# Issuing the tensor engine's fp32 transposes as transpose operations in a two-block transformer kernel

## The chip, the cores and the metric

One NeuronCore of one Trainium2 chip runs the whole program; the other cores are idle. The metric is the device time in microseconds (us), the median over several executions.

## What is computed

The reference chains two small transformer programs over 256 tokens of width 1024, batch 1, all in fp32. The first has a gated delta rule layer and then a layer of sparse attention with three branches (compressed, selected and window keys); the second has a stick-breaking attention, a gated linear recurrence and two MLPs with squared ReLU. Cut to the order of the work:

```python
def first_block(x, c, ...):
    h = rmsnorm(x, norm_g[0]) * (1 + scale) + shift
    x = x + gate * gated_deltanet_layer(h, ...)
    shared = nsa_shared_kv(x, ...)
    h = rmsnorm(x, norm_g[1]) * (1 + scale) + shift
    x = x + gate * nsa_layer(h, shared, rel_bias, ...)
    return rmsnorm(x, final_g)

def second_block(x, ...):
    x = x + stick_breaking_attention(rms_norm(x, g0), w_qkv, w_o)
    x = x + squared_relu_mlp(rms_norm(x, g1), w1, w2)
    x = x + rglru_block(rms_norm(x, g2), ...)
    x = x + squared_relu_mlp(rms_norm(x, g3), w1, w2)
    return rms_norm(x, norm_final)
```

In `nsa_layer` each of 16 heads computes, in two branches, scores q kᵀ plus a bias, a masked softmax p and the product p v. At 256 tokens the selected branch sees every block and the window covers the sequence, so both are plain causal attention over 256 keys.

## The kernel before

The tokens lie on partitions in two tiles of 128. Every weight matrix is streamed from HBM in blocks of 1 MB (128 x 2048 fp32) through three raw buffers. ScalarE writes a rounded high part (L537, `split_hi`) and VectorE the remainder (L994, `split_lo`), into two split buffers; every weight product is then three TensorE products, high by high, high by low and low by high (`passes`, L1576, whose products are recorded at L1579 to L1581). A `feature_block` has 48 such products of 256 columns, a pair of `token_blocks` calls 48 of 512 columns. Each engine runs its own program in a fixed order written out by hand, and the engines meet at counting semaphores; there is no planner.

**Transposes.** `transpose` (L1573) is used for all of them: it is a matmul with the data as the stationary operand and the fp32 identity as the moving one. The calls are:

- `transposes(call)` (L1626), ten times: the normalised activations `xn` (2 x 128 x 1024) become feature-major in four PSUM banks, 16 transposes of 128x128. The first token tile's eight wait for the first `xn_ready`, the second tile's eight for the second. As the pairs of the second tile end (`tr_done`), ScalarE writes the high part hT_hi (`transposed_hi`, L561, recorded at L571, L578 or L580), VectorE the remainder hT_lo (`transposed_lo`, L1036, recorded at L1042 or L1048, and L1063), and the weight products wait for hT_lo (`fresh`, L1594). The calls are named h0, y0, kv, h1, y1, sb, o2, m0, rg and m1.
- in the delta rule stage, for each of two groups of four heads, 8 of v, 4 of k and 8 of the matrices `ddT` (L1727, L1735, L1746), in all 40.
- 4 small ones of `few` (L1676), 4 of `hid_rows` (L1852) and 4 of the compressed branch's weights `pc` (L1936).
- `weights_T(h)` (L1904): 6 of 128x128 for each of the 16 heads of the sparse attention, 96 in all: the exponentials `pr` become `pT`.

That is 160 + 40 + 12 + 96 = 308 transposes.

**The sparse attention's turn.** TensorE does for head h, in this order: the scores of head h + 1 (`scores`, L1892, recorded at L1900 and L1901, 64 partitions deep), the transposes of head h, and the products p v of head h - 1 (`head_out`, L1915, recorded at L1927 to L1929, 64 columns wide). Meanwhile VectorE adds the bias to the scores and takes the row maximum (L1342, L1345), ScalarE the exponentials (L801, `p_ready`); after the transposes ScalarE copies the first branch's result (L810) and VectorE the second's (L1385) to SBUF.

```python
for h in range(BH):
    if h + 1 < BH:
        scores(h + 1)
    weights_T(h)
    if h >= 1:
        head_out(h - 1)
```

Of the kernel before, what the change touches and what calls it, by code (L numbers as in the profile page):

```python
# [205 lines left out]
def build(nc, I, O):  # L206
# [11 lines left out]
    with ExitStack() as ctx:  # L218
# [1350 lines left out]
        def _(pe):  # L1569
            taken = [0]  # L1570
            dt32 = nc.tensor.matmul

            def transpose(out, x, one):  # L1573
                return dt32(out, x, one, start=True, stop=True)  # L1574

            def passes(out, lhs, rhs, first, last):  # L1576

# [48 lines left out]
            def transposes(call):  # L1626

                for m in range(MT):
                    pe.wait_ge(S["xn_ready"], XN[call] - 1 + m)
                    for g in range(4):  # L1630
                        bank = TR_BANK[g]
                        for c in range(2):
                            k = 2 * g + c
                            ins = transpose(bank[:, c * T + m * P:c * T + (m + 1) * P], xn[:, m, k * P:(k + 1) * P], ident)
                        if m == MT - 1:
                            ins.then_inc(S["tr_done"], 1)
# [30 lines left out]
            def few_columns(call, n):  # L1667

                _, hi, lo = take()
                for k in range(KC):  # L1670
                    fresh(call, k)
                    ins = passes(G[0][0:n, 0:T], (hi[:, k, :], lo[:, k, :]), hT(k), k == 0, k == KC - 1)
                ins.then_inc(S["w_used"], 1)
                pe.wait_ge(S["few"], 1 if call == "h0" else 2)
                for m in range(MT):
                    ins = transpose(G[1][:, m * n:(m + 1) * n], few[0:n, m * P:(m + 1) * P], ident[0:n, 0:n])  # L1676
                ins.then_inc(S["few_T"], 1)
# [38 lines left out]
            for hg in range(2):  # L1716
# [8 lines left out]
                for m in range(MT):  # L1725
                    for h in range(4):
                        ins = transpose(quad(X[m])[:, h, :], vT[:, 4 * hg + h, m * P:(m + 1) * P], ident)  # L1727
                    ins.then_inc(S["v_tok"], 1)
# [113 lines left out]
            for b in range(6):  # L1842
# [12 lines left out]
                if b == 1:  # L1855
# [7 lines left out]
                    for g in range(BG):  # L1863
                        for j in range(2):
                            ins = dt32(TB[1][0:NCMP, g * HD:(g + 1) * HD], hid[1][:, j, g * NCMP:(g + 1) * NCMP], cw2[1][:, j, :],
                                       start=(j == 0), stop=(j == 1))
# [261 lines left out]
```

## Time and profile before

| what | us |
|---|---|
| median of 3 runs | 1271.9 (1269.74 to 1272.17) |
| span of the profiled execution, first to last instruction | 1274.7 |
| the profiled execution's own time | no other than its span is recorded |
| TensorE matmuls busy | 1148.2 (90%) |
| TensorE weight loads busy | 1032.5 (81%) |
| VectorE busy | 701.8 (55%) |
| ScalarE busy | 567.5 (45%) |
| TensorE clock granted, mean | 0.936 of full |

Busy times are of one profiled execution. Matmuls overlap each other in the records, so their busy time is not the engine's throughput: that is read from start to start. A product of fp32 data is recorded as two weight loads and two matmuls, a product of the split parts as one of each, so the 308 transposes are 616 records. The granted clock is 1.00 at 2.4 GHz and 0.50 at 1.2 GHz.

### The profile page before, as it was taken

How to read it: one execution, taken by the hardware profiler on the slowest of the kernel's cores; microseconds unless marked ns; L12 is line 12 of the kernel's file. 1: busy time of each engine (PE TensorE's matmuls, PEld its weight loads, DVE VectorE, ACT ScalarE, POOL GpSimd, SP SyncE). 2: the span in 40 equal slices, each digit the busy share in tenths (PEclk: the TensorE clock that was granted, in tenths of full speed). 3: DMA queues.
4: the chain of work that ended last, by engine and by line, in shares of the span. 5: the costliest groups of instructions: out<-in, count | busy, mean ns of one | idle time of the engine just before them, and what ended most of it. 6: DMA issues, size and time to landing. Idle time of an engine off the chain costs nothing. (4 is left out here: it accounts for less than half of the span.)

```text
span 1274.7 us, 17755 instructions
## 1 busy us (share of the span) xinstructions
PE 1148.2 (90%) x7548; PEld 1032.5 (81%) x7548; DVE 701.8 (55%) x983; ACT 567.5 (45%) x837; POOL 90.1 (7%) x87
## 2 busy tenths in 40 slices
PE   2799978786989999998799998999999988999997
PEld 2699878785878786787599677989897976999896
DVE  5598455557544564355634345554555766654544
ACT  3354342323544443243543454434435585444343
POOL 1000016160000000031000001000000010000000
PEclk9798989897989997698999799999999998999999
DMA  9755405052335774000335303455556425455551
GB/s 328 226 165 167 133 11 188 2 198 71 102 103 169 236 255 166 1 1 1 111 109 179 131 1 113 144 178 195 182 183 197 133 99 165 135 197 180 186 197 66
DMA packets 118319, 178.45 MB, mean 140 GB/s; under 512 B 5125, under 2 KB 77987, under 8 KB 118241
## 3 DMA queue, kind: packets, MB, share of 16 engines
q1 hardware_dynamic: 116736, 172.40, 41.6%
q0 software_dynamic: 1088, 2.96, 0.7%
q10 hardware_dynamic: 416, 1.97, 0.4%
q8 instruction: 59, 0.97, 0.3%
q14 instruction: 20, 0.16, 0.0%
HBM read 176.27 MB, written 1.05 MB: 139 GB/s over the span
## 5 line engine op out<-in xcount | busy, mean ns | idle before, releaser
L994 DVE TENSOR_TENSOR sb_w_lo<-sb_raw,sb_w_hi 128x2048 fp32r<-128x2048 f32 (+2 forms) x141 | 319.4, 2265 | 348.9 <-ACT sb_w_hi L537 348.7
L537 ACT ACTIVATE sb_w_hi<-sb_raw 128x2048 fp32r<-128x2048 f32 (+2 forms) x141 | 266.1, 1888 | 177.9 <-PE G L1581 166.1
L1579 PE MATMUL X<-sb_hT_hi,sb_w_hi 128*128 128x256 f32 x1056 | 303.7, 288 | 3.0 <-DVE sb_hT_lo L1048 2.3
L1580 PE MATMUL X<-sb_hT_lo,sb_w_hi 128*128 128x256 f32 x1056 | 301.5, 285 | 0.0
L1581 PE MATMUL X<-sb_hT_hi,sb_w_lo 128*128 128x256 f32 x1056 | 301.4, 285 | 0.0
L1579 PEld LDWEIGHTS X<-sb_hT_hi,sb_w_hi 128*128 128x128 f32 x1056 | 205.2, 194 | 4.9 <-issue 4.1
L1580 PEld LDWEIGHTS X<-sb_hT_lo,sb_w_hi 128*128 128x128 f32 x1056 | 205.1, 194 | 0.6
L1581 PEld LDWEIGHTS X<-sb_hT_hi,sb_w_lo 128*128 128x128 f32 x1056 | 205.0, 194 | 0.0
L1579 PE MATMUL G<-sb_w_hi,sb_hT_hi 128*128 128x512 f32 x288 | 114.8, 398 | 10.2 <-DVE sb_hT_lo L1533 9.2
L1580 PE MATMUL G<-sb_w_lo,sb_hT_hi 128*128 128x512 f32 x288 | 113.5, 394 | 0.0
L1581 PE MATMUL G<-sb_w_hi,sb_hT_lo 128*128 128x512 f32 x288 | 113.5, 394 | 0.0
L1581 PE MATMUL G<-sb_w_hi,sb_uT_lo 128*128 128x512 f32 x256 | 101.1, 395 | 0.0
L1580 PE MATMUL G<-sb_w_lo,sb_uT_hi 128*128 128x512 f32 x256 | 101.1, 395 | 0.0
L1579 PE MATMUL G<-sb_w_hi,sb_uT_hi 128*128 128x512 f32 x256 | 101.0, 395 | 0.0
L1579 PEld LDWEIGHTS G<-sb_w_hi,sb_hT_hi 128*128 128x128 f32 x288 | 54.9, 191 | 23.0 <-issue 11.1
L868 ACT ACTIVATE sb_ur<-X 128x512 f32<-128x512 f32 x32 | 19.1, 598 | 106.5 <-PE X L1581 106.5
L1581 PEld LDWEIGHTS G<-sb_w_hi,sb_hT_lo 128*128 128x128 f32 x288 | 54.8, 190 | 11.6
L1580 PEld LDWEIGHTS G<-sb_w_lo,sb_hT_hi 128*128 128x128 f32 x288 | 55.0, 191 | 11.1
L1574 PE MATMUL T<-sb_consts,sb_xn 128*128 128x128 f32 x160 | 31.0, 356 | 32.2 <-DVE sb_xn L1023 20.8
L1581 PEld LDWEIGHTS G<-sb_w_hi,sb_uT_lo 128*128 128x128 f32 x256 | 48.2, 188 | 11.2
L1580 PEld LDWEIGHTS G<-sb_w_lo,sb_uT_hi 128*128 128x128 f32 x256 | 48.3, 188 | 10.7
L1579 PEld LDWEIGHTS G<-sb_w_hi,sb_uT_hi 128*128 128x128 f32 x256 | 48.3, 189 | 10.6
(346 smaller groups left out, 1682.9 us busy)
## 6 DMA issues: line engine op xcount, KB each, us to landing
sb_raw<-in_mlp_w SPq DMA_DIRECT2D x64, 1024.0 KB, 5.3
sb_raw<-in_ada_w SPq DMA_DIRECT2D x24, 1024.0 KB, 5.1
sb_raw<-in_a_in_w SPq DMA_DIRECT2D x16, 1024.0 KB, 5.9
sb_raw<-in_b_in_w SPq DMA_DIRECT2D x16, 1024.0 KB, 5.4
sb_raw<-in_sb_w_qkv SPq DMA_DIRECT2D x12, 1024.0 KB, 5.1
sb_raw<-in_rg_w_in SPq DMA_DIRECT2D x8, 1024.0 KB, 5.3
sb_raw<-in_a_out_w SPq DMA_DIRECT2D x4, 1024.0 KB, 4.9
sb_raw<-in_b_out_w SPq DMA_DIRECT2D x4, 1024.0 KB, 5.2
```

The costliest lines, as they stand in the source:

```text
L537: nc.scalar.activation(w_hi[s][:, 0:nk * w], raw[b % RAW_SLOTS][:, 0:nk * w], ACT.Copy).then_inc(S["w_hi"], 1)
L868: nc.scalar.activation(ur[b % 2][:, :, :], X[(f0 + b) % 2][:, :].rearrange("p (c t) -> p c t", c=2), ACT.Relu).then_inc(S["fm_out"], 1)
L994: nc.vector.tensor_tensor(w_lo[s][:, 0:nk * w], raw[b % RAW_SLOTS][:, 0:nk * w], w_hi[s][:, 0:nk * w].bitcast(F32), ALU.subtract).then_inc ...
L1574: return dt32(out, x, one, start=True, stop=True)
L1579: dt32(out, lh, rh, start=first, stop=False)
L1580: dt32(out, lh, rl, start=False, stop=False)
L1581: return dt32(out, ll, rh, start=False, stop=last)
```

## The change

The helper issues the tensor engine's transpose operation, with the same output, the same data and the same identity. Nothing else differs: the order, the waits, the buffers, and the copies out of PSUM.

```diff
--- before.py
+++ after.py
@@ -1571,7 +1571,7 @@
             dt32 = nc.tensor.matmul
 
             def transpose(out, x, one):
-                return dt32(out, x, one, start=True, stop=True)
+                return nc.tensor.transpose(out, x, one)
 
             def passes(out, lhs, rhs, first, last):
 
```

## Rows read from the trace of the kernel before

**Rows 1.** The page: span, and each engine's busy time.

```profile
span 1274.7 us, 17755 instructions
...
PE 1148.2 (90%) x7548; PEld 1032.5 (81%) x7548; DVE 701.8 (55%) x983; ACT 567.5 (45%) x837; POOL 90.1 (7%) x87
```

**Rows 2.** The instructions of line 1574: count, shortest/median/longest in ns, first and last start.

```profile
L1574 PE MATMUL T<-sb_consts,sb_pr x192: 274/276/581, 515.5 to 591.6; 128*128 128x128 f32 x192
...
L1574 PE MATMUL T<-sb_consts,sb_xn x160: 275/377/582, 31.9 to 1083.8; 128*128 128x128 f32 x160
...
L1574 PE MATMUL T<-sb_consts,sb_pc x8: 420/421/566, 500.8 to 502.5; 128*120 128x128 f32 x8
```

**Rows 3.** Busy time by stretch, line 1574 alone: stretch, length, PE, PEld, clock, DMA.

```profile
0.00:1274.70 1274.70, 100.95 (x616) 94.17 (x616) 0.94 0.43 140
```

**Rows 4.** Busy by stretch, sparse attention: length, PE, PEld, DVE, ACT, POOL, clock, DMA.

```profile
512.90:533.40 20.50, 20.50 (x79) 17.65 (x79) 5.78 (x30) 6.70 (x27) 0.00 (x0) 0.50 0.00 1
533.40:547.00 13.60, 13.60 (x103) 12.23 (x102) 8.32 (x39) 4.47 (x18) 2.41 (x2) 1.00 0.01 2
...
550.50:553.90 3.40, 3.40 (x19) 3.40 (x17) 0.56 (x2) 2.23 (x9) 0.00 (x0) 0.50 0.00 0
553.90:594.50 40.60, 39.27 (x296) 35.40 (x295) 21.96 (x103) 18.37 (x73) 11.45 (x12) 1.00 0.00 1
```

**Rows 5.** The same stretches, line 1574 alone: length, PE, PEld, clock, DMA.

```profile
512.90:533.40 20.50, 8.78 (x36) 7.90 (x36) 0.50 0.00 1
...
553.90:594.50 40.60, 14.42 (x108) 12.73 (x108) 1.00 0.00 1
```

**Rows 6.** TensorE's matmuls in order of time, two turns: start, length, operation, count.

```profile
521.25 2.93 PE L1574 MATMUL T<-sb_consts,sb_pr 128*128 128x128 f32 x12
523.97 0.53 PE L1927 MATMUL X<-sb_vtok,sb_pT 128*128 128x64 f32 x2
...
526.56 0.79 PE L1900 MATMUL G<-sb_kdup,sb_qB 64*128 64x128 f32 x2
...
529.42 2.93 PE L1574 MATMUL T<-sb_consts,sb_pr 128*128 128x128 f32 x12
...
573.12 1.60 PE L1574 MATMUL T<-sb_consts,sb_pr 128*128 128x128 f32 x12
...
577.44 1.61 PE L1574 MATMUL T<-sb_consts,sb_pr 128*128 128x128 f32 x12
```

**Rows 7.** Busy by stretch, stick-breaking attention's start; columns as in rows 4.

```profile
714.00:735.00 21.00, 19.36 (x58) 13.84 (x58) 7.09 (x11) 9.39 (x16) 0.00 (x0) 0.51 0.20 68
```

**Rows 8.** Order of time: products of split parts, 128x128 by 128 columns, ten in a row.

```profile
352.10 0.28 PE L1581 MATMUL X<-sb_w_hi,sb_hT_lo 128*128 128x128 f32 x1
...
353.11 0.28 PE L1581 MATMUL X<-sb_w_hi,sb_hT_lo 128*128 128x128 f32 x1
```

**Rows 9.** Order of time: the bf16 products of 16 columns at the start.

```profile
22.08 7.03 PE L1646 MATMUL G<-sb_rbx,sb_hot 97*128 97x16 bf16 x256 [22.08 <-DVE sb_rbx L1082]
```

**Rows 10.** Order of time: the transposes of call y0 and what surrounds them.

```profile
301.02 2.36 DVE L1222 TENSOR_TENSOR sb_xn<-sb_xn,sb_zs 128x1024 f32<-128x1024 f32 x2
...
302.30 2.08 PE L1574 MATMUL T<-sb_consts,sb_xn 128*128 128x128 f32 x8 [6.00 <-DVE sb_xn L1222]
...
305.88 1.92 PE L1574 MATMUL T<-sb_consts,sb_xn 128*128 128x128 f32 x8
307.04 1.63 ACT L578 ACTIVATE sb_hT_hi<-T,sb_params 128x256 fp32r<-128x256 f32 x4 [8.37 <-PE T L1574]
...
309.00 0.47 PE L1579 MATMUL G<-sb_w_hi,sb_hT_hi 128*128 128x512 f32 x1
```

**Rows 11.** Busy by stretch, columns as in rows 4: y0, then products after a pause.

```profile
304.70:308.10 3.40, 3.40 (x18) 3.40 (x18) 2.21 (x4) 1.06 (x3) 1.01 (x2) 0.50 0.43 132
308.10:311.50 3.40, 3.32 (x18) 2.72 (x18) 3.40 (x9) 2.03 (x6) 0.00 (x0) 0.99 0.56 217
1055.60:1059.00 3.40, 3.40 (x8) 2.72 (x9) 2.94 (x5) 2.35 (x3) 0.00 (x0) 0.50 0.68 266
```

## The prediction

> **What bounds the kernel now.** I read the page first: TensorE has 1148.2 us of recorded matmul in a span of 1274.7, far ahead of VectorE and ScalarE [rows 1]. So a shorter TensorE instruction is worth something wherever TensorE isn't waiting. The view of line 1574 gives the transposes: the 128x128 ones last 275 ns at their shortest, and the calls on xn have a median of 377 ns, so many of them run at the lower clock [rows 2]. All 616 records hold 100.95 us [rows 3]. That is the size of the prize; the question is how much of it is on the path, and what else these records do.
>
> The largest piece is the sparse attention, 512.9 to 594.5, 81.6 us with 192 of the records. TensorE is recorded busy nearly without a break, VectorE and ScalarE are busy about half the time or less [rows 4]: TensorE bounds it. The same rows show the second thing to see. In its first 20.5 us TensorE is busy for all 20.50, and yet the granted clock is 0.50, 1.2 GHz; then it is 1.00, falls once, and stays at 1.00 to the end. One turn (a head's transposes, the products of the head before, the scores of the head after) takes 529.42 - 521.25 = 8.17 us at the low level and 577.44 - 573.12 = 4.32 at the high one [rows 6]. The clock is worth more here than the transposes.
>
> **What one transpose costs.** Now: 12 records from 521.25 to 523.97, so 2.72 / 6 = 0.453 us per transpose at the low level; at the high level 1.60 us less the 0.275 of the last record, over 11 steps, is 0.12 per record, 0.24 per transpose [rows 6, 2]. The operation itself stands nowhere in this trace. The nearest rows are the products of split parts with the same 128x128 operand of four-byte data and the same 128 columns, one record each: ten in a row start 1.01 / 9 = 0.112 us apart, at the high clock [rows 8]. The low end is the bf16 products, 7.03 / 256 = 0.027 [rows 9]; the high end is 0.24, no change (nothing excludes a price above it, but no row suggests one). I take the nearest row, one record per transpose: 0.112 high, 0.225 low, so 0.227 us saved at the low level and about 0.12 at the high one.
>
> The Trainium skill (TensorE: Matmul & The Clock Gate, Terms) says that a transpose mode makes fp32 four times faster; an estimate by it is 0.113 low and 0.06 high, and would put my time some 11 us lower. No row here shows it.
>
> **The clock in the attention.** What raised it? Not recorded busy time: it was full for 20.5 us at 0.50 [rows 4]. The stick-breaking attention, which has no transposes but the same kind of products, 64 partitions deep or 64 columns wide, likewise runs 21 us at 0.51 with TensorE busy for 19.36 [rows 7]. In the sparse attention the rise at 533.4 comes just after the transposes that begin at 529.42 [rows 4, 6], the only products of the turn that are both 128 deep and 128 wide, 2.72 of its 8.17 us. In call y0 the clock is 0.50 through the transposes and 0.99 right behind them [rows 11]. My reading is that the transposes, as ordinary matmuls, are what brings the clock up in these places. After the change they last half as long and stream fewer passes; what is left of a low turn (2.59 us of narrow products from 523.97 to 526.56, 2.86 of shallow ones to 529.42) is what kept the clock down in both stages. The stage starts low today, so I expect it to stay low to its end.
>
> At the low level the turn becomes 8.17 - 6 x 0.227 = 6.81 us. The stage holds 16 transpose groups, 16 groups of products and 15 of scores: 16 x 6.81 - 2.86 = 106.1, against 81.6 now: **+24.5**. The exponentials can't bind at such a turn: VectorE and ScalarE have 5.78 and 6.70 us of work in 20.5 us [rows 4].
>
> The Trainium skill (the same page, Part 4: PE-mode transpose) says that the full clock does not engage for transpose mode, which does not count as busy in the same way; by it the +24.5 stands whatever the operation's length. It is the rule that speaks against this change, and no run here shows it yet.
>
> **The ten calls on xn.** In y0 the second tile's xn is ready at 303.39, but its transposes start at 305.88, behind the first tile's [rows 10]. After the change the first eight end at 302.30 + 8 x 0.225 = 304.10, hT_hi starts at 304.10 + (1.16 - 0.45) = 304.8 in place of 307.04, and the chain to the first product at 309.00 moves with it: 2.2 us. The bound for any low call is 10 x 0.227 = 2.3, for a high one 1.2. Six calls start at the low level (y0, kv, y1, sb, m0, rg); I take 1.8 each, because in some the second tile's xn or a weight split on ScalarE comes later. o2 and m1, high, give 0.8 each, h0 and h1 nothing: they wait for the modulation or the split. Sum -12.4.
>
> Against that, in these six the first product now finds the clock up [rows 11]; the transposes did the warming. Where products start cold, at 1055.60, they stay at 0.50 for 3.4 us [rows 11], and half of that, 1.7, is lost. Where the first ones come one by one behind hT_lo they may lose more; I take 2.3 each, 13.8. In o2 and m1 the clock is up today because transposes bridge the pause before the products; a shorter bridge may let it fall, and I charge 1.5 each. Together 16.8 - 12.4: **+4.4**. So the calls, which look like the safe part, give back what they gain.
>
> **The rest.** The four transposes of pc are at the low level [rows 2], on the path: -0.9. The 40 of the delta rule stage save up to 2 us where TensorE is waited for, and cost as much where the product levels behind ddT then start low: 0, within 2. The eight of few and hid_rows are not worth a term. No DMA, wait or queue moves. SP's weight prefetch is three buffers deep and follows the splits; where TensorE is later it only gains slack.
>
> **Sum.** 24.5 + 4.4 - 0.9 = +28.0 on the profiled execution, 1274.7 to 1302.7 of span. That execution is 2.8 us over the median of the runs; the same +28.0 on 1271.9 gives 1299.9, so 1300.
>
> **Rivals.**
>
> *The clock doesn't care (faster).* The mechanism is TensorE's path alone: shorter transposes at the clock pattern of today. Of 192 records 36 are in the first stretch [rows 5]: 18 x 0.227 + 78 x 0.12 = 13.5 us in the attention, 12 after turns that then wait for the exponentials; 12.4 in the calls, 0.9 and 2 elsewhere: 27.3 less, 1244.6. It decides if the attention reaches and holds 1.00, that is, if its turns fall under 4 us. For it: the clock did hold at 1.00 for 40.6 us, where transposes are 14.42 of 39.27 us busy [rows 4, 5], not the larger part. Against it: rows 4 and 7 at 0.50 with TensorE full. The Trainium skill (Perfetto Trace Analysis, Transposes) advises the transpose over a matmul; that is this rival's view. Chance 0.14. A milder form, the attention up but the calls paying as above, gives -12 + 4.4 - 0.9 = -8.5, 1263.4; chance 0.10.
>
> *The operation takes as long as now and the clock follows as now:* no change, 1271.9, chance 0.06. This is also the case that the operation is the same product under another name.
>
> *As long as now, but without the effect on the clock (much slower):* 16 x 8.17 - 2.86 = 127.9, +46.3, and 16.8 in the calls: 1335. Chance 0.04.
>
> The forecast has 0.66. Its own range: with the bf16 price at the low level, 0.055, the turn is 8.17 - 2.72 + 0.33 = 5.78 and the stage 89.6 (+8.0), the calls give another us or so each, and the whole is about 1275; the other end is the 1335. Inside these I hold 1280 to 1320 for it.
>
> **How the numbers follow.** A difference under 0.2%, 2.5 us, can't be told from none. Slower 0.66 + 0.04 = 0.70, same 0.06, faster 0.24. To leave out no more than 2 in 10 the range must take in the fast rival: 1243 to 1320.
>
> **What would show it.** Line 1574 with 308 records in place of 616, and steps of about 0.11 and 0.22 us. The attention at 0.50 from end to end, with turns of 6.8 us and a length near 106. The first product of the six calls 1 to 2 us sooner after xn, but at 0.50. The MLP stretches unchanged. I am wrong if the attention's clock reaches 1.00 and stays: then the turn is near 3.7 and the time near 1245 to 1263. I am also wrong in the terms, if not in the sign, if a transpose's step isn't 0.11.

## The result, and the profile after

| | before | after |
|---|---|---|
| median of 4 runs, beside each other | 1272.0 us (1269.7 to 1272.4) | 1282.8 us (1279.2 to 1285.8) |
| ratio | | 1.0111, interval 1.0064 to 1.0159 |
| span of the profiled execution | 1274.7 us | 1284.0 us |
| granted clock, mean | 0.936 | 0.900 |

The change makes the kernel slower by 1.1%, about 11 us. The sign and the place are those forecast; the amount is less than half of the 28 us. The four runs of the kernel before that stand beside it lie at its usual median; in other runs it took down to 1260 us (below), and against those the same change costs 21 us.

The page of the changed kernel, its span and busy times:

```profile
span 1284.0 us, 17139 instructions
...
PE 1148.2 (89%) x7240; PEld 1025.2 (80%) x7240; DVE 699.8 (55%) x983; ACT 567.1 (44%) x837; POOL 90.1 (7%) x87
```

308 records fewer than in [rows 1], and the same busy time to the tenth: what the shorter transposes took away, a slower clock put back. Line 1574 in it (count, shortest/median/longest in ns, first and last start):

```profile
L1574 PE MATMUL T<-sb_consts,sb_pr x96: 272/421/478, 505.1 to 601.5; 128*128 128x128 f32 x96
...
L1574 PE MATMUL T<-sb_consts,sb_xn x80: 272/421/477, 31.7 to 1092.6; 128*128 128x128 f32 x80
...
L1574 PE MATMUL T<-sb_consts,sb_pc x4: 421/421/470, 493.5 to 494.2; 128*120 128x128 f32 x4
```

Half as many records as in [rows 2], and the median of the attention's 96 went from 276 to 421 ns: they run at the low level now. The stretches of the attention (length, PE, PEld, DVE, ACT, POOL, clock, DMA):

```profile
503.60:509.60 6.00, 4.50 (x28) 3.51 (x29) 3.20 (x19) 2.90 (x12) 0.00 (x0) 1.00 0.00 0
509.60:606.50 96.90, 96.90 (x381) 84.44 (x380) 34.55 (x164) 31.13 (x125) 17.17 (x18) 0.50 0.00 1
```

It begins at the high level, unlike [rows 4]; after 6 us the clock falls, and stays at 0.50 for all the 96.9 us that are left, TensorE busy for every one of them. One turn there, TensorE's matmuls in order of time:

```profile
521.92 1.54 PE L1574 MATMUL T<-sb_consts,sb_pr 128*128 128x128 f32 x6
523.25 0.53 PE L1927 MATMUL X<-sb_vtok,sb_pT 128*128 128x64 f32 x2
...
525.84 0.79 PE L1900 MATMUL G<-sb_kdup,sb_qB 64*128 64x128 f32 x2
...
528.70 1.54 PE L1574 MATMUL T<-sb_consts,sb_pr 128*128 128x128 f32 x6
```

A transpose is (523.25 - 521.92) / 6 = 0.222 us, half of the 0.453 of [rows 6], and the turn 528.70 - 521.92 = 6.78 us in place of 8.17. Yet the stage, from the scores of head 1 to the last product p v, takes 102.9 us in place of 81.5, because before most turns ran at the high level in 4.32.

### The profile page after: what moved, and what is told of

Read it like the earlier page. It is cut to its first block and busy times, and to the rows that moved or that the text cites. A ratio compares the mean times of both kernels' runs of the same rounds, so it can differ in the third digit from the quotient of the medians.

```text
span 1284.0 us, 17139 instructions
## 1 busy us (share of the span) xinstructions
PE 1148.2 (89%) x7240; PEld 1025.2 (80%) x7240; DVE 699.8 (55%) x983; ACT 567.1 (44%) x837; POOL 90.1 (7%) x87
## 5 line engine op out<-in xcount | busy, mean ns | idle before, releaser
L1579 PEld LDWEIGHTS X<-sb_hT_hi,sb_w_hi 128*128 128x128 f32 x1056 | 208.6, 198 | 8.7 <-issue 8.0
L1580 PEld LDWEIGHTS X<-sb_hT_lo,sb_w_hi 128*128 128x128 f32 x1056 | 208.6, 197 | 0.6
L1581 PEld LDWEIGHTS X<-sb_hT_hi,sb_w_lo 128*128 128x128 f32 x1056 | 208.2, 197 | 0.0
L801 ACT ACTIVATE sb_pr<-sb_pr,sb_nmx 128x128 f32<-128x128 f32 x64 | 28.3, 443 | 69.7 <-DVE sb_nmx L1345 69.6
L1580 PEld LDWEIGHTS G<-sb_w_lo,sb_uT_hi 128*128 128x128 f32 x256 | 48.2, 188 | 10.7
```

Source lines behind the costliest of these rows:

```text
L801: ins = nc.scalar.activation(pr[h % 2][:, br, sl_], pr[h % 2][:, br, sl_], ACT.Exp, bias=nmx[:, h % 2, i:i + 1], accum_out=esum[:, h, br, ...
L1579: dt32(out, lh, rh, start=first, stop=False)
L1580: dt32(out, lh, rl, start=False, stop=False)
L1581: return dt32(out, ll, rh, start=False, stop=last)
```

## The experiments

The first four kernels ran on one chip, the next four on another, the last four on a third, each time beside the kernel before, whose medians there were 1271.1, 1265.0 and 1271.4 us. Its single runs spread from 1260 to 1279, which is why the intervals below are wide; the last experiments ask why.

### The attention's 96 as products, all else as in the change

```diff
 def transpose(out, x, one):
     return nc.tensor.transpose(out, x, one)
+def product(out, x, one):
+    return dt32(out, x, one, start=True, stop=True)
...
-                        ins = transpose(TB[br][:, i * P:(i + 1) * P], ...)
+                        ins = product(TB[br][:, i * P:(i + 1) * P], ...)
```

> The change everywhere but in the 96 transposes of the sparse attention, which stay matmuls. If the attention's loss is the clock (my theory), the clock is low for some 20 us of the stage and then 1.00, the stage is 75 to 83 us long, and the time is what the other transposes alone give: 11.8 us ahead of the kernel before outside the attention in the changed kernel's trace, so about 1260. If the loss is the length or the switching of the operation itself somewhere else (rival), the time stays above 1272.

Measured: 1253.0 us (1251.7 to 1254.0), ratio 0.9868 [0.9807, 0.993]. With the change undone at one line of it, the kernel is not only 30 us faster than the changed one, but faster than the kernel before. Its stage, in one stretch:

```profile
500.40:573.00 72.60, 69.29 (x503) 62.25 (x504) 39.32 (x183) 34.02 (x136) 17.17 (x18) 0.98 0.00 1
```

The clock is 0.98 over the stage. So the whole loss, and more, lies in the attention's transposes. I had expected a stage that starts low and takes 75 to 83 us, and 1260 us in all; it began at the high level, with a first turn of 3.88 us, and took 72.6.

### The attention's 96 alone as the operation

```diff
 def transpose(out, x, one):
-    return nc.tensor.transpose(out, x, one)
+    return dt32(out, x, one, start=True, stop=True)
...
-                        ins = transpose(TB[br][:, i * P:(i + 1) * P], ...)
+                        ins = nc.tensor.transpose(TB[br][:, i * P:(i + 1) * P], ...)
```

> Only the 96 transposes of the sparse attention are transpose operations. My theory: the stage stays at 0.50 to its end, 103 to 107 us, 21 to 25 more than before, and the time is 1292 to 1297. The rival, that the calls on xn and what they do to the clock matter as much, gives 1280 or less.

Measured: 1298.4 us (1297.2 to 1300.5), ratio 1.0226 [1.0155, 1.0298]: +27 us on the median of the kernel before. The stage (same columns):

```profile
511.90:617.20 105.30, 105.27 (x408) 90.79 (x408) 37.83 (x183) 34.00 (x136) 17.15 (x18) 0.50 0.00 1
```

This is the stage that the prediction worked out: entered at the low level, low from end to end, 105.3 us where 106.1 was forecast. The two runs add up about: 27 us for the 96, and 1271.1 - 1253.0 = 18 us gained by the other 212, against the median beside them, leave 9, and the whole change costs 11. Both figures move with the spread of the kernel before.

### The changed kernel, each of the 96 issued twice

```diff
-                        ins = transpose(TB[br][:, i * P:(i + 1) * P], ...)
+                        for _ in range(2):
+                            ins = transpose(TB[br][:, i * P:(i + 1) * P], ...)
```

The second writes the same values over the first. 

> The changed kernel with each of the 96 transposes issued twice, so the transposes of a turn are again as long as before the change. If the operation counts for the clock as a matmul of its length does, the clock rises in the stage as in the kernel before (stage about 80, time about 1260). If the operation does not raise the clock at all (the rival that the skill's rule gives), all turns stay at 0.50 and take 8.1 us each, the stage 127, the time about 1307.

Measured: 1249.7 us (1245.5 to 1250.5), ratio 0.9834 [0.9765, 0.9904]. The stage, and one turn of it in order of time (the added line moves the numbers of those below by one):

```profile
497.40:567.60 70.20, 66.56 (x504) 59.45 (x504) 39.55 (x183) 34.01 (x136) 17.18 (x18) 1.00 0.01 1
```

```profile
511.28 1.53 PE L1574 MATMUL T<-sb_consts,sb_pr 128*128 128x128 f32 x12
512.64 0.33 PE L1928 MATMUL X<-sb_vtok,sb_pT 128*128 128x64 f32 x2
...
515.53 1.53 PE L1574 MATMUL T<-sb_consts,sb_pr 128*128 128x128 f32 x12
```

Twice the transposes, 33 us less. The clock is 1.00 through the stage, and the turn is 4.25 us. I had expected a stage of 80 us and a time of 1260; the stage was entered at the high level and kept it. This is the run that settles how the operation acts on the clock. It differs from the changed kernel in nothing but more of the same operation; if transpose operations weren't counted as work by whatever grants the clock, adding them could not hold it up. They do count. What failed in the changed kernel is their number: six a turn, beside the same narrow and shallow products, left the clock at 0.50, and twelve held it at 1.00. (The rule of the Trainium skill, "TensorE: Matmul & The Clock Gate", Part 4, that the full clock does not engage for transpose mode, is not what this run shows for fp32 transposes; the measurement decides.) The twelve operations take 1.53 us and the twelve records of six products took 1.60 [rows 6]: an operation costs what one record did.

### Fillers in three heads

```diff
+                if 2 <= h < 5:
+                    for i in range(8):
+                        dt32(TB[i % 2][:, 3 * P:4 * P], ident, ident, start=True, stop=True)
                 for br in range(2):
```

Eight products of the identity with itself, of which nothing is used, ahead of the transposes of heads 2, 3 and 4. 

> The changed kernel with 8 more 128x128 fp32 products of the identity by itself ahead of the transposes of heads 2, 3 and 4, their results unused. They should bring the clock to 1.00 by head 3 or 4. If the high level then holds by itself, as it did before the change, a turn falls to 3.7 us, the stage to about 79 and the time to about 1259. If the shorter transposes can't hold it, the clock falls again a few turns later, the stage is 105 to 112 and the time 1285 to 1292.

Measured: 1276.9 us (1272.9 to 1281.3), ratio 1.0057 [1.0017, 1.0097].

```profile
501.40:517.70 16.30, 14.76 (x70) 12.81 (x71) 5.13 (x29) 6.33 (x26) 0.00 (x0) 0.69 0.00 1
517.70:538.10 20.40, 18.48 (x142) 16.61 (x140) 11.72 (x51) 8.24 (x33) 5.71 (x6) 1.00 0.01 1
538.10:600.40 62.30, 62.30 (x249) 54.61 (x247) 22.23 (x104) 19.57 (x78) 11.44 (x12) 0.50 0.00 1
```

The fillers bring the clock up at 517.7. Without them one turn runs at the high level, in 3.54 us; at 538.1 the clock falls and doesn't come back. The stage is 98.9 us, and the time 1276.9, between the two outcomes expected, nearer to the second. So six operations a turn neither keep the high level for long nor bring it back: this is no matter of how the stage is entered. One thing stands beside it: TensorE pauses just ahead of the fall, for 1.92 us until its transposes at 537.11 may start.

```profile
537.11 0.85 PE L1574 MATMUL T<-sb_consts,sb_pr 128*128 128x128 f32 x6 [1.92 <-ACT sb_pT L810]
```

The same turn has a pause in other kernels too (1.27 us in the run with each issued twice, where the clock stays at 1.00), and the kernel before loses the level for 3.4 us soon after this turn and gets it back. So the pause may have set the moment of the fall; that the clock stays down for the 62.3 us after it, in turns of 6.78 us, it doesn't explain.

### The calls on xn alone

```diff
-                            ins = transpose(bank[:, c * T + m * P:...], xn[:, m, ...], ident)
+                            ins = nc.tensor.transpose(bank[:, c * T + m * P:...], xn[:, m, ...], ident)
```

This is made in the kernel before. 

> The kernel before with the transpose operation on the 160 transposes of xn alone; the attention's 96 and all others stay products. Theory after the first four runs (a call keeps what its shorter transposes give, because after them the first weight products find the clock up as before, or up sooner): about 12 us under the kernel before, 1.5 at most of it given back in the stretch before the attention; ratio about 0.991, and the lag at the last product before the attention about -8. Rival, my forecast's step (the shorter transposes no longer warm the clock, 16.8 paid for 12.4 gained): 4.4 us over, ratio 1.003, with the low stretches after the calls 2 to 3 us longer each. The sparse attention in both: turns of 8.17 us at the low level and 4.3 at the high one, a stage between 72.6 (entered high) and 81.6 (entered low).

Measured: 1264.0 us (1259.4 to 1264.7), ratio 0.9965 [0.9925, 1.0004]. Neither value came, and against a kernel before that spreads by 19 us the run doesn't separate them. Its trace does show my forecast's price, behind five of the calls (y0, kv, sb, m0 and rg). Behind call y0:

```profile
304.70:308.10 3.40, 1.54 (x6) 1.07 (x5) 3.36 (x8) 2.60 (x8) 0.49 (x1) 0.50 0.71 180
308.10:311.50 3.40, 3.40 (x10) 2.64 (x10) 3.40 (x5) 0.00 (x0) 0.00 (x0) 0.58 0.45 172
```

TensorE is full from 308.10 with weight products, and the clock is 0.58; before it was 0.99 in that stretch [rows 11]. In the changed kernel the same place looks like this (y0 in order of time, then the clock around it):

```profile
299.30 2.36 DVE L1222 TENSOR_TENSOR sb_xn<-sb_xn,sb_zs 128x1024 f32<-128x1024 f32 x2
...
302.34 1.06 PE L1574 MATMUL T<-sb_consts,sb_xn 128*128 128x128 f32 x4
...
303.07 1.57 ACT L578 ACTIVATE sb_hT_hi<-T,sb_params 128x256 fp32r<-128x256 f32 x4 [6.13 <-PE T L1574]
...
306.12 0.47 PE L1579 MATMUL G<-sb_w_hi,sb_hT_hi 128*128 128x512 f32 x1 [1.86 <-DVE sb_hT_lo L1048]
```

```profile
301.00:304.80 3.80, 3.25 (x16) 2.85 (x14) 3.80 (x4) 1.73 (x5) 2.04 (x3) 0.50 0.09 25
304.80:308.20 3.40, 2.08 (x9) 1.77 (x10) 3.37 (x9) 1.31 (x4) 0.00 (x0) 1.00 0.94 316
```

Here the short transposes bring the clock up before the first product, as the long ones did. From the start of the first xn to the first product it is 306.12 - 299.30 = 6.82 us, and 309.00 - 301.02 = 7.98 before [rows 10]. Behind call sb the same two kernels differ. The first of sb's weight products starts at 643.43 before the change and at 651.66 after it (same columns, first line before, second line after):

```profile
642.60:646.00 3.40, 3.39 (x27) 3.22 (x27) 3.04 (x8) 2.02 (x6) 0.00 (x0) 0.99 0.00 0
651.20:654.60 3.40, 2.94 (x14) 2.97 (x15) 2.66 (x7) 1.60 (x5) 0.00 (x0) 0.50 0.00 0
```

Here the short transposes leave the clock low, and the first 48 product records take 7.90 us in place of 5.96. Over all the traces of this document: in the ten with the operation in the calls, kv and m0 pay such a price in all (7.8 to 8.0 us in place of 6.0), rg in nine, sb in five, y0 in two, m1 in one, y1 at most 0.8 us and o2 nothing; in the four without it none pays. So the price is real in kv, m0 and rg nearly always, and in y0 and sb it depends on the execution or on what ran before.

### Nine operations a head, two ways

The second branch's three issued twice; and, in another kernel, all six issued twice in heads 0, 2, 4 and so on.

```diff
+                        for _ in range(1 + br):        # the one kernel
+                        for _ in range(2 - h % 2):     # the other
```

> The changed kernel in which the three transposes of the second branch are issued twice: nine operations a head in place of six or twelve, the same results. If the clock follows a share of the turn (theory: what counts is how much dense 128x128 work a turn holds, whatever it is called), nine may or may not do. Holding: turns near 3.9 us, a stage near 65 to 68 and a time near 1244. Not holding: turns of 8.17 - 3 x 0.227 = 7.5 us at the low level, a stage near 115 and a time near 1292. A mixture of both levels would lie between, as in the run with fillers in three heads (98.9 us).

> The changed kernel in which every second head (0, 2, 4 ...) issues its six transposes twice: the same 144 operations in all as with the second branch twice, but in twelves and sixes. If a mean over turns decides, it does as that run does. If each turn stands for itself, the clock falls in the single turns and rises in the double ones: a stage between 85 and 105 us. If it holds high throughout: turns of 4.25 and 3.54 in turn, a stage near 63 to 66 and a time near 1242.

Measured: 1254.3 us, ratio 0.9877 [0.9795, 0.9959], and 1247.8 us (1245.7 to 1248.8), ratio 0.9825 [0.9756, 0.9895]. Of the four runs with the second branch twice three took 1253.6 to 1254.8 us at a mean clock of 0.932 to 0.940; the fourth took 1272.8 at 0.920, and no trace of it is kept, so whether its attention lost the level isn't known. The second branch twice:

```profile
508.00:525.50 17.50, 17.50 (x75) 15.59 (x74) 5.17 (x23) 6.46 (x27) 0.00 (x0) 0.51 0.00 1
525.50:576.00 50.50, 47.33 (x357) 42.06 (x356) 29.55 (x141) 25.25 (x101) 17.15 (x18) 1.00 0.01 1
```

Every other head twice:

```profile
500.50:515.50 15.00, 15.00 (x67) 12.88 (x65) 5.53 (x30) 6.40 (x27) 0.00 (x0) 0.54 0.00 0
515.50:572.60 57.10, 52.62 (x382) 46.78 (x381) 33.59 (x153) 27.73 (x110) 17.16 (x18) 0.97 0.01 1
```

Both fall to the low level at first and then come back by themselves, which six a turn never did, with no dense work in the stage but the operation. Then they hold, but for one stretch of 3.4 us in the second: most turns take 3.9 us in the one, 3.88 and 4.22 in the other. The stages are 73.7 and 74.0 us, longer than the 63 to 68 expected, by the low part. A turn with six operations can thus stay at the high level if its neighbours hold twelve: each turn doesn't stand for itself.

### Every head twice, again, with five rounds

> The same kernel as in the run with every head's transposes issued twice, now beside the calls alone and with five rounds: 0.983 of the kernel before again, a stage near 70 us at the high level from its start. Were the first result a chance of how the stage was entered, the stage would start at the low level here, with turns of 8.2 us, and take 80 or more.

Measured: 1250.3 us (1248.7 to 1251.1), ratio 0.9845 [0.9789, 0.9902]. The stage, at the high level from its start:

```profile
500.60:570.70 70.10, 66.49 (x503) 59.38 (x504) 39.55 (x183) 34.01 (x136) 17.16 (x18) 1.00 0.01 1
```

### The kernel before, two more traces

> The kernel before, unchanged, for one more trace. Its runs on the last two chips fall in two groups, 1260 to 1263 us and 1270 to 1279, with nothing between but one at 1265; the granted clock is 0.95 in the first and 0.934 to 0.941 in the second. Theory: the groups differ in the level at which the sparse attention is entered. In a run of the first group its stage is then near 72 us, with turns of 4.3 from the first on, against the 81.5 and turns of 8.17 of the profile we have; the rest lies in the call before it. Rival: the groups differ elsewhere (the projections, the gated recurrence) and the attention starts low in both.

> The same once more, so that both groups have a chance to be seen; same expectations as the look before it.

Measured: 1260.0 and 1260.5 us, spans 1258.1 and 1258.6, clock 0.95. Both are 16 us under the execution that the prediction worked from, with the same instructions. The stage of the first of them:

```profile
504.30:512.00 7.70, 7.68 (x29) 6.19 (x29) 1.93 (x10) 2.23 (x9) 0.00 (x0) 0.57 0.00 0
512.00:580.90 68.90, 66.36 (x477) 60.27 (x476) 37.38 (x173) 31.90 (x127) 17.17 (x18) 0.95 0.01 1
```

It too is entered low, but is up after one set of transposes, not after three [rows 4]: 76.5 us in place of 81.5. The clock around a set can thus rise at once or two sets later, in the same program. My theory (entered high, 72 us) missed; the level at the entry isn't the difference. The larger part, 8.5 us, lies ahead of the attention, in low stretches that these executions don't have or have shorter. On the third chip two of eleven runs lay at 1265 and 1267, so the two groups aren't sharp either.

### The changed kernel and the products in the heads, again

> The changed kernel once more, five rounds, beside the two others. Theory: it has one group of times only, near 1283, since its attention falls to the low level however it is entered; 1.018 of the kernel before's first group and about 1.007 of the second. Its stage is 103 to 106 us with turns of 6.8. Rival: it too has a group in which the level is held, with turns of 3.5 and a stage near 60, and then a time near 1240 shows up among its runs.

> The operation everywhere but in the attention's 96, again with five rounds beside the changed kernel. 1253 again, one group of times only (the calls' shorter transposes let the attention be entered at the high level), 30 us under the changed kernel and 7 under the first group of the kernel before. If those 7 us were only chance of the chip, it would equal the first group, 1260.

Measured: 1281.6 us (1279.2 to 1285.9), ratio 1.0103 [1.006, 1.0145], and 1253.9 us (1248.5 to 1260.2), ratio 0.9877 [0.9828, 0.9925]. The low part of the stage in the changed kernel, and the stage with products:

```profile
503.50:601.50 98.00, 97.55 (x385) 85.11 (x386) 34.89 (x167) 32.13 (x128) 17.16 (x18) 0.51 0.00 1
```

```profile
503.20:575.80 72.60, 69.28 (x503) 62.25 (x504) 39.31 (x183) 34.01 (x136) 17.16 (x18) 0.98 0.00 1
```

The products in the heads came again, but not in one group: five of the six runs took 1248.5 to 1254.8 us, one 1260.2. All ten runs of the changed kernel lie between 1279 and 1286: nothing near 1260 or 1240 shows, and in both traces its attention falls to the low level. Against the kernel before at 1260 it is 21 us slower, against its runs at 1271 to 1279 some 3 to 10.

### The traces in one table

The start of head 1's scores, the length of the stage from there to the start of the last product p v, and from there to the end of the last matmul:

| kernel | attention begins | stage | the rest |
|---|---|---|---|
| before, three traces | 512.8, 504.3, 504.8 | 81.5, 76.5, 76.6 | 673.1, 669.9, 669.9 |
| the 96 alone | 511.9 | 105.2 | 673.1 |
| the calls alone | 509.1 | 76.5 | 669.9 |
| changed, two traces | 503.6, 498.6 | 102.9, 102.9 | 670.1, 670.1 |
| the 96 as products, two | 500.4, 503.2 | 72.6, 72.6 | 669.7, 669.8 |
| the 96 twice, two | 497.4, 500.6 | 70.1, 70.1 | 668.7, 668.8 |
| second branch twice | 502.3 | 73.7 | 668.6 |
| every other head twice | 498.6 | 74.0 | 667.0 |
| fillers in three heads | 501.4 | 98.9 | 667.3 |

The column "attention begins" moves without the change too: the stretch from the start to the delta rule's first transposes of v takes 164.1 to 168.8 us in the fourteen traces, in kernels of either kind.

## Why the prediction was right, and where it was off

**The price of the operation: right.** 0.222 us at the low level (0.225 forecast); at the high level (1.53 - 0.27) / 11 = 0.115 in the run with each issued twice (0.112 forecast). One record at the price of one record of a product was the right nearest row. The four times that the Trainium skill ("TensorE: Matmul & The Clock Gate", Terms) states for fp32 is not seen: against a product with the identity it is 0.453 to 0.222, two times.

**The attention: right in place, sign and nearly in size.** +24.5 forecast, 102.9 - 81.5 = +21.4 measured. The turn of 6.81 us came as 6.78. The 3.1 us between are the first two turns, of 3.88 and 6.17, run wholly or in part at the high level; I had the stage entered low. The 96 alone, entered low, gave 105.3 against 106.1. The reason given, that dense transposes are what brings the clock up, stands after the filler and the doubled ones. That the narrow and shallow products do little for the clock is read from stretches where they fill most of a turn at 0.50; no run added or removed any. The rule that I set beside it, which would make it a matter of the operation's kind, does not stand. I also wrote that by that rule the +24.5 holds whatever the operation's length; that is wrong on my own figures, for at the low level a shorter operation shortens the stage, to +8.0 at the bf16 price.

**The calls: this is the step that failed.** I wrote that "in these six the first product now finds the clock up [rows 11]; the transposes did the warming", priced the loss of that at 16.8 us, and put +4.4 for the ten calls. Between the profiled executions the eight calls that had a term moved like this, in us: first the time from the last product ahead of the call (in y0 from the start of the first xn) to its first product, then the time of the first 48 product records.

| call | to the first product | first 48 records | together |
|---|---|---|---|
| y0 | -1.2 | 0.0 | -1.2 |
| kv | -1.5 | +2.1 | +0.5 |
| y1 | -2.2 | 0.0 | -2.2 |
| sb | -1.8 | +1.9 | +0.1 |
| o2 | -1.2 | 0.0 | -1.2 |
| m0 | -2.8 | +2.0 | -0.8 |
| rg | -0.5 | +1.9 | +1.4 |
| m1 | -0.6 | 0.0 | -0.6 |

The gain, 12.4 in my sum, is 11.8. The loss, 16.8 in my sum, is 7.9: four of the six low calls pay, 2 us each, near the 2.3 that I took, and there the first products run at 0.50 as I wrote; y0 and y1 pay nothing, because their short transposes still bring the clock up before the first product, and o2 and m1, which I charged 1.5 each for a pause, pay nothing either. So the ten calls give -4.0 in place of +4.4. What sets y0 and y1 apart from the other four was not tried.

**What the one execution hid.** The rest of the miss is 28.0 - 9.3 - 8.4 - 3.1 = 7.2 us, nearly all ahead of the attention, where the sum had -0.9 for pc and nothing for the delta rule stage. There the changed kernel was 9.2 us ahead. But two other executions of the kernel before are 8.0 and 8.5 us ahead there too. The kernel before may begin its attention anywhere from 504 to 513; those nine traces in which every transpose ahead of the attention is the operation begin at 497.4 to 503.6, median 500.6. So a gain there exists, for the ranges don't touch (503.6 and 504.3 are their nearest ends), but of its size the profiled pair says little. Part of it can be placed. From the last product ahead of call h1 to the attention it is 148.8 us in the profiled execution before and in the 96 alone, 144.5 and 144.6 in the other two traces of before, 144.6 with the calls alone, and 141.9 to 142.1 in the nine. So of the 6.9 us that the profiled pair shows there, 4.2 are low stretches that come and go between executions of the same code, and 2.7 are steady and come with the small transposes (of few, hid_rows and pc), which the calls alone leave as products; the sum had 0.9 for pc and no term for the others. The -4.0 of the calls holds up: against the other two traces of before the same eight sum to -3.2. The 3.0 us that the changed kernel gains from the attention's end to the end of the program don't: these two traces take 669.9 us there, the changed kernel 670.1.

**The rivals.** The fast one, that the clock doesn't care, was wrong for the 96, which alone cost 27 us where it had them gain 12, and near in time for the other 212, though four calls show that the clock does care: it had 12.4 + 0.9 + 2 = 15.3 us for them, and 18 by the medians was measured (7 against the kernel before at its shortest, 1260). I had its two halves paired the wrong way: the milder form let the attention gain and the calls pay. Why the attention pays in every turn and a call at most once can be read from the traces: behind kv, sb, m0 and rg the clock is low for 4.6 to 5.0 us of dense weight products and then 1.00, while in the attention nothing dense follows a head's transposes. It was not tried by a run of its own.

**Luck.** The total came nearer to the forecast, or farther, by the draw of the kernel before: +10.7 us on the medians, +21 against its runs at 1260. The sign doesn't hang on it.

## What to carry to other kernels

A TensorE instruction has two effects, its time and what it does for the clock. Where a loop alternates dense 128x128 work with narrow or shallow products and its clock isn't steady, read what raises it before making the dense part shorter: here half the transpose work cost 21 us in a stage of 82, and issuing the operation twice won 11 (26 and 6 against the two traces of before whose stage is 76.5). Keep the long form, or issue the operation more often, in a loop whose clock the transposes carry, and use the operation elsewhere; the versions with the operation outside the attention and products, doubled or half-doubled operations in it all came to 0.983 to 0.988 of the kernel before, too near each other to rank, each beside a kernel before that spreads itself (every other head twice has the lowest median, 1247.8 us).

And one profiled execution of a kernel whose clock moves is one draw: the same program gave spans of 1258.1 and 1274.7 us, and a change's lag behind it, stretch by stretch, carries that spread.

## What was not expected of the hardware

- Issuing each of the 96 transposes twice is 33 us faster than once (1249.7 against 1282.8), with the granted clock 1.00 against 0.50 in the stage.
- A level that the stage has reached isn't kept by what follows: after three heads with fillers the clock was 1.00 for 20.4 us and then 0.50 for 62.3, with TensorE busy for all of the 62.3.
- Transposes half as long leave the first weight products behind four calls at 0.50 (48 records in 7.8 to 8.0 us in place of 6.0), and behind two others not.
- The same program spreads by 18 to 19 us (1260 to 1279) on each of three chips, and its granted clock goes with it, 0.953 to 0.934. The changed kernel's spread is 7.
